# A hybrid decoder layer on eight cores: earlier norms, constant matmuls during the first load, and attention steps placed by estimated readiness

## What is computed

```python
h = rmsnorm(x, g_mix_pre); proj = h @ w_in
a_val, a_gate, q, k, v, f_logit = split(proj)
u = causal_depthwise_conv(a_val * sigmoid(a_gate), conv_w, conv_b)   # width 31
conv_out = silu(layernorm(u))
log_f = log_sigmoid(f_logit + b_forget); c = cumsum(log_f)
attn = softmax(q k^T / 8 + c_t - c_s, causal) @ v                    # 8 heads x 64
mix = concat(conv_out, attn) @ w_out
x = x + rmsnorm(mix, g_mix_post)
h = rmsnorm(x, g_ffn_pre)
y = (silu(h @ w_gate) * (h @ w_up)) @ w_down
x = x + rmsnorm(y, g_ffn_post)
```

## Time and profile before

| | |
|---|---|
| median of 3 runs | 2523.05 us (2521.86 to 2574.8) |
| the profiled execution | 2522.89 us |
| its span on the slowest core, 4 | 2521.3 us; the others 2503.7 to 2517.0 us |
| mean granted TensorE clock | 0.965 to 0.969 of 2.4 GHz |

### The profile page before, as it was taken

How to read it: one execution, slowest core, us unless ns; L and a number is a source line. 1 busy time by engine, 2 the same in 40 slices (tenths; PEclk the granted TensorE clock), 3 DMA queues, 4 the chain that set the end, 5 groups by cost and what they waited for, 6 DMA issues and landing times.

```text
span 2521.3 us, 53550 instructions; the slowest of 8 cores (2503.7 to 2521.3 us)
## 1 busy us (share of the span) xinstructions
PE 2282.3 (91%) x19680; PEld 1046.8 (42%) x19680; DVE 1064.8 (42%) x1645; ACT 1576.5 (63%) x1393; POOL 542.7 (22%) x901
## 2 busy tenths in 40 slices
PE   6888889999899779998999999999999899999895
PEld 2343434444344334443444444444444444444342
DVE  3545454455344543344234424424424332443643
ACT  2156567777676666676677677777767767772311
POOL 0231223132121421141013023013113201302301
PEclk9899999999899979999999999999999999998998
DMA  6765657577566765666635644554553464453542
GB/s 146 184 150 138 175 125 199 126 158 158 126 179 147 147 155 122 191 136 189 191 108 150 200 129 137 181 160 127 179 179 110 139 205 115 141 167 122 171 143 91
DMA packets 225324, 384.28 MB, mean 152 GB/s; under 512 B 34736, under 2 KB 152752, under 8 KB 222896
## 3 DMA queue, kind: packets, MB, share of 16 engines
q1 hardware_dynamic: 191840, 296.52, 40.5%
q0 software_dynamic: 33232, 84.34, 16.4%
HBM read 350.19 MB, written 72.55 MB: 168 GB/s over the span
## 4 chain that ended last, share of the span: by engine, by line
PE 67%; ACT 11%; DVE 7%; issue 6%; DMA 4%; POOL 2%; SPq 1%; DVEq 0%; ACTq 0%; POOLq 0%
PE pbig L372 67%; ACT s_pt L1076 5%; DVE s_tmp L860 2%; SPq L344 1%; ACT L384 1%; DVE s_x L862 1%; DMA s_xs<-xT 1%; DMA s_kr<-k_s 1%; ACT s_rstd L384 1%; DVE s_hT L465 1%; ACT s_sq L478 1%; ACT s_pt L1081 1%; DMA conv_s<-s_cvst 1%; DMA v_s<-s_vst 0%; POOL s_pt L1085 0%
## 5 line engine op out<-in xcount | busy, mean ns | idle before, releaser
L1076 ACT ACTIVATE s_pt<-pbig,s_bias 128x2048 bf16<-128x2048 f32 x512 | 1005.9, 1965 | 440.2 <-PE pbig L372 434.2
L372 PE MATMUL pbig<-s_h,s_wr 128*128 128x512 bf16 x2816 | 697.4, 384 | 11.5 <-DVE s_sa L908 10.8
L372 PEld LDWEIGHTS pbig<-s_vr,s_pt 128*128 128x128 bf16 x8832 | 349.3, 99 | 166.8 <-issue 50.9
L372 PE MATMUL pbig<-s_vr,s_pt 128*128 128x65 bf16 x8832 | 371.4, 195 | 18.9 <-DVE s_atok L1116 8.6
L372 PEld LDWEIGHTS pbig<-s_h,s_wr 128*128 128x128 bf16 x2816 | 245.5, 98 | 335.6 <-issue 116.4
L372 PE MATMUL pbig<-s_qr,s_kr 64*128 64x512 bf16 x1024 | 312.9, 386 | 77.5 <-ACT s_pt L1076 56.1
L908 DVE SCALAR_TENSOR_TENSOR s_sa<-s_th,pbig 128x512 f32<-128x512 f32 x176 | 120.8, 686 | 491.4 <-ACT s_th L907 487.4
L372 PE MATMUL pbig<-s_qw,s_kr 64*128 64x512 bf16 x1024 | 314.4, 388 | 0.0
L1085 POOL TENSOR_SCALAR_AFFINE_SELECT s_pt<-s_pt 128x128 bf16<-128x128 bf16 x256 | 84.9, 331 | 929.5 <-ACT s_pt L1081 904.1
L372 PE MATMUL pbig<-s_actA,s_wr 128*128 128x512 bf16 x1024 | 256.9, 381 | 1.5 <-DVE s_mix L941 1.1
L409 POOL TENSOR_TENSOR s_ssA<-s_ssA,s_sqr 128x512 f32<-128x512 f32 x112 | 154.9, 1383 | 459.9 <-ACT s_sqr L402 455.6
(11 more groups left out here) (142 smaller groups left out, 2274.5 us busy)
## 6 DMA issues: line engine op xcount, KB each, us to landing
s_wr<-wg_b SPq DMA_DIRECT2D x88, 512.0 KB, 3.9
s_wr<-wu_b SPq DMA_DIRECT2D x88, 512.0 KB, 4.4
s_wr<-wd_b SPq DMA_DIRECT2D x128, 352.0 KB, 3.2
s_vr<-v_s SPq DMA_DIRECT2D x288, 130.0 KB, 3.4
s_kr<-k_s SPq DMA_DIRECT2D x448, 64.0 KB, 3.9
s_xs<-xT POOLq DMA_DIRECT2D x48, 512.0 KB, 6.5
...
```

The source lines that it names most:

```text
L372: P.op("pe", lambda e: e.matmul(out, lhsT=lhsT, rhs=rhs, start=start, stop=stop, **kw), reads=reads, writes=[wkey])
L1076: P.op("act", lambda e: e.activation(out=p[:], in_=pbig[:, 0:4, :], func=AF.Exp, bias=bias[:, c, h:h + 1], scale=1.0), reads=bk + bias.key ...
```

## The change

The planner gets a model of time. `_Cost` is a stand-in engine with a duration for each kind of instruction (for example 512 / 2400 + 0.0025 us for a full-size bf16 matmul at one clock, 0.08 + columns / 1200 us for an activation). `_time` gives each recorded instruction an end from its engine's last end and its dependences' ends, each DMA a landing from one shared wire, 1.28 us for a change between Ln and Tanh on ScalarE and 0.097 us for a change of matmul kind. `ready` gives the time at which the dependences of keys are met:

```diff
+    def ready(self, eng, reads, writes):
+        t = 0.0
+        for d in self._deps(eng, reads, writes):
+            if d.is_dma:
+                t = max(t, self.landed[d.semkey])
+            elif d.eng != eng or eng != "pe":
+                t = max(t, d.done)
+        return t
```

A filler group yields 0.0 first, with its readiness in `fneed`; an attention step does the same in `need`. The loop uses both:

```diff
+    fneed = []
     def group(nk, lhs, rhs, out, reads, b, cost=MM, step=4):
+        fneed[:] = [lambda: max(max(P.ready("pe", reads(k), ()) - cost * k for k in range(nk)), P.ready("pe", (), [PB(b)]))]
+        yield 0.0
         for k in range(nk):
             mm(out, lhs(k), rhs(k), k == 0, k == nk - 1, reads(k), PB(b))
```

```diff
                 for c in range(2 * j + 2):
+                    n = hpos[(j, h)] % NQ
+                    if c <= 2 * j:
+                        need[:] = [kring[upos[(j, h, c // 2)] % NKV].keys + qtwin[n].keys + qring[n].keys, [PB(i) for i in range(4)]]
+                    else:
+                        need[:] = [kdring[n].keys + qring[n].keys, [PB(i) for i in range(3)]]
+                    yield 0.0
                     yield qk(j, h, c)
                     if len(pend) > 1:
+                        p = pend[0]
+                        need[:] = [p[3].keys + vring[upos[(p[0], p[1], p[2] // 2)] % NKV].keys, [PB(4)]]
+                        yield 0.0
                         d = pv()
...
+        if c == 0.0:
+            t = fneed[0]()
+            while fa[2] > -DEBT and t > P.free["pe"] + 0.15 and need and P.ready("pe", need[0], need[1]) < t - 0.3:
+                s = a_step()
+                if s is None:
+                    break
                 fa[2] -= s
             continue
         if isinstance(c, tuple):
...
         rem_f = max(A_END * f_total - fa[0], 1.0)
         rate = min(R_MAX, (a_total - fa[1]) / rem_f)
-        fa[2] = min(fa[2] + rate * c, 2.0)
+        fa[2] = min(fa[2] + rate * c, CAP)
         while fa[2] > 0:
+            if need and fa[2] < CAP - 0.3 and P.ready("pe", need[0], need[1]) > P.free["pe"] + 0.1:
+                break
             s = a_step()
             if s is None:
                 fa[2] = 0
```

Constant matmuls during the first load, chunk 0's norm written out, and norms of chunks 1 to 3 inside `p_kv(i)`, after the third V group (EARLY = 2):

```diff
+    def norm_early(i):
         flush("sq")
         b = bank()
         yield from stats(sq, 8, b)
         norm_tail(b, rstd, 1.0 / D)
-        defer("h", [scale_by(xs, V_GPRE, rstd, hT[i % 3], k) for k in range(8)], 2, every)
+        def one(k):
+            def f():
+                scale_by(xs, V_GPRE, rstd, hT[i % 3], k)()
+                if k % 2 and i < 3:
+                    x_piece(i + 1, k // 2, "sp")
+            return f
+        defer(("h", i), [one(k) for k in range(8)])
+        if i == 3:
+            defer("x", [lambda g=g: bulk.append(("x", lambda: x_piece(4, g))) for g in range(4)], 6, 2)
...
-        flush("h")
+        b = bank()
+        hold = Rot(4)
+        def idle(n):
+            for _ in range(n):
+                h = hold.next()
+                mm(pb[h][:], ones_bf[:], pt[0][:, 0, :], True, True, ones_bf.keys + pt[0].keys, PB(h))
+        idle(8)
+        for k in range(8):
+            P.op("act", lambda e, k=k: e.activation(out=sq[:, k, :], in_=xs[:, k, :], func=AF.Square), reads=[xs.keys[k]], writes=[sq.keys[k]])
+            mm(pb[b][:], ones_bf[:], sq[:, k, :], k == 0, k == 7, ones_bf.keys + [sq.keys[k]], PB(b))
+            idle(10 if k == 2 else 2 if k < 7 else 8)
+        norm_tail(b, rstd, 1.0 / D)
+        for k in range(8):
+            scale_by(xs, V_GPRE, rstd, hT[0], k)()
         load_x(1)
         ld("pool", identb, identb[:], cst_d[:, 0, :])
         yield from p_kv(0)
-        yield from norm_fin(1)
-        flush("h")
...
-        yield from norm_fin(2)
-        flush("h")
-        load_x(3)
-        wl("q", winQ, 0, C_Q, C_K, hT[2].keys[7:8])
-        wl("g", winG, 0, 0, C_Q, hT[2].keys[7:8])
+        flush_h(2)
+        wl("q", winQ, 0, C_Q, C_K, hT[2].keys[0:1])
+        wl("g", winG, 0, 0, C_Q, hT[2].keys[0:1])
...
+            if hp == 3 and i < 3:
+                norm_sq(i + 1)
...
+            if tb == EARLY and i < 3:
+                yield from norm_early(i + 1)
```

The first FFN chunk (j = 0) takes eight bf16 squares to TensorE for both norms; its residual has g_mix_post already in mix:

```diff
+            if j == 0:
+                P.op("dve", lambda e, b=b, ob=ob: e.tensor_scalar(out=mix[:, ob, :], in0=pb[b][:], scalar1=V(V_GPOST + ob), scalar2=None, op0=ALU.mult),
+                     reads=[PB(b)] + vecs.keys, writes=[mix.keys[ob]])
+                P.op("act", lambda e, b=b, ob=ob: e.activation(out=sq[:, ob, :], in_=pb[b][:], func=AF.Square), reads=[PB(b)], writes=[sq.keys[ob]])
+                continue
...
+        yield from stats(*((sq, 8, b) if j == 0 else (hlA, 2, b)))
         norm_tail(b, rstd, 1.0 / D)
-        defer("x1", [resid(mix, V_GPOST, X, ob) for ob in range(8)], 2, 1 if j == 0 else 2)
-        defer("x1", sq_steps(X, 8, ssA, hlA), 4, 1 if j == 0 else 2)
+        if j == 0:
+            def first(ob):
+                eng, T = ("pool", ssV) if ob > 5 else ("dve", tmp[ob % 2])
+                def f():
+                    P.op(eng, lambda e: e.tensor_tensor(out=T[:], in0=mix[:, ob, :], in1=rstd[:], op=ALU.mult), reads=[mix.keys[ob]] + rstd.keys, writes=T.keys)
+                    P.op(eng, lambda e: e.tensor_tensor(out=X[:, ob, :], in0=T[:], in1=X[:, ob, :], op=ALU.add), reads=T.keys + [X.keys[ob]], writes=[X.keys[ob]])
+                return f
+            def square(k):
+                return lambda: P.op("act", lambda e: e.activation(out=sq[:, k, :], in_=X[:, k, :], func=AF.Square), reads=[X.keys[k]], writes=[sq.keys[k]])
+            defer("x1", [first(ob) for ob in (0, 6, 1, 2, 7, 3, 4, 5)], 1)
+            defer("x1", [square(k) for k in range(8)], 4)
+            return
+        defer("x1", [resid(mix, V_GPOST, X, ob) for ob in range(8)], 2, 2)
+        defer("x1", sq_steps(X, 8, ssA, hlA), 4, 2)
...
+        yield from A3(0)
         yield ("att", 2.0)
-        yield from A3(0)
-        yield ("att", 3.0)
         for j in range(NOWN):
```

For the last own chunk the V staging is a smaller buffer, vst2, with 8 instead of 12 blocks, 4 instead of 8 decay steps, and its store is shorter; sqr and ssA are now outside it:

```diff
-    vst = [OV("vst0", [128, NH, 12, 65], BF16, w4), OV("vst1", [128, NH, 12, 65], BF16, tmp[0])]
-    ust.append(OV("ust2", [128, CH], BF16, hlA, 1, 1024))
-    assert hlA.off + 1024 >= vst[1].off + vst[1].size
+    vst = [OV("vst0", [128, NH, 12, 65], BF16, w4), OV("vst1", [128, NH, 12, 65], BF16, tmp[0]), OV("vst2", [128, NH, 8, 65], BF16, tmp[0])]
+    ust.append(OV("ust2", [128, CH], BF16, ssA, 1, 1024))
+    assert ssA.off + 1024 >= vst[1].off + vst[1].size and sqr[0].off >= vst[2].off + vst[2].size
+    vst_of = lambda j: vst[0 if j == 0 else 2 if j == NOWN - 1 else 1]
```

141 lines of the change are left out of this document (106 added, 35 removed).

## The result

The changed kernel takes 2467.14 us (median of 4 runs, 2463.09 to 2468.23), the kernel before 2521.86 us (3 runs, 2520.8 to 2523.05): ratio 0.978, 95% interval 0.9761 to 0.9799. That is faster, 55 us of the 99 forecast. It is inside the range, outside the likeliest case (2400 to 2455), and 3 us under the window of rival (a). In some executions of these kernels (one of the kernel before, 2574.8 us) the cores of one half of the chip, or all eight, had a lower mean granted clock, down to 0.80, and took up to 12% longer; times and ratios here are those of the other executions, of which e5 and e8 have one each and so no ratio.

What follows compares the result with a forecast made beforehand. TensorE, busy 91%, was taken as the bound, with only its idle time and low clock to win. Terms -11 - 28 - 42 - 13 - 19 - 4 + 2.7 + 15 = -99 gave 2424 us from 2522.9; range 2372 to 2484.

Steps and rivals of the forecast that it cites:

- rival (a): Planner's picture of time drifts, part 4 only trades one wait for another: 2470 to 2485 us, chance 0.21.
- Parts 1 and 2: Start of the kernel: constant matmuls plus early norms for chunks 1 to 3, -11 us (bounds -3 to -15).
- Part 2: Early norms, chunks 1 to 3: -5.4 us, -0.6 for clock, and -3.5 from a V evacuation wait that goes.
- The constant matmuls: During the first load: higher clock for the three stats matmuls and first groups, -1.5 us (bounds +1 to -3).
- Part 3: First FFN chunk: v_s store wait gone, shorter A2 to A3 chain, fewer forced attention units; -28 us, 60% of 47.
- Part 4 in the own chunks: Attention by readiness in 100:850: half of 84.1 us idle and of 27 us clock, -42 and -13 us.
- Part 4 in the FFN: Attention by readiness in 1000:2280: 40% of 48 us idle, -19 us, and -4 us of clock.
- The penalty: +15 us for what the planner cannot know: low clock, late loads, attention put ahead of a truly ready group.
- (b): Rival: readiness does nearly all, upper bounds throughout, no penalty; 135 us saved, 2388 us, chance 0.14.
- (c): Rival: put-off steps pile up before a chunk's need mark, where no filler runs; slower, 2573 us, chance 0.04.
- (d): Rival: a denser TensorE draws a lower clock, and the gain is given back; 2583 us, chance 0.01.
- What would show it: Signs: idle before 2280 about 115 us, s_pt waits below 45, stats within 14 us after the A2 tail, among others.

Runs made afterwards that it cites:

- e5: The changed kernel without the constant matmuls during the first load: 2467.17 us (one run).
- e8: The changed kernel with a credit cap of 12 instead of 4, so more attention steps may be put off: 2488.35 us (one run).
- e6: The changed kernel with norms of chunks 1 to 3 between the chunks again and the old order of loads: 2474.82 us, ratio 0.9825.
- e7: The changed kernel with the first FFN chunk's norms and residual as before, freed buffers kept: 2456.56 us, ratio 0.9698.
- e12: The changed kernel with the large V staging buffer and its overlay as before, new norms kept: 2466.17 us, ratio 0.979.
- e10: The changed kernel with full attention steps' exponentials over 1024 of 2048 columns, half the probabilities left out: 2390.43 us, ratio 0.9438.
- e1: The changed kernel with both readiness rules off and the credit cap back at 2.0: 2500.24 us, ratio 0.9879.

## Why the prediction was right, and where its sizes were off

**What bounds the kernel** held. TensorE's busy time changed by 5.6 us (2282.3 to 2276.7), with some 9.4 us of constant matmuls added (92.1 us busy to own chunk 0, 82.6 in e5), so on the other work it fell by 15; the gain is in idle time and clock.

**Parts 1 and 2** (-11) gave 6.6. Part 2 is right in mechanism and gave some 6 of its 9.5 (e6). The constant matmuls (-1.5) gave nothing (e5): the step that failed is that the higher clock would last into the 24 matmuls that nothing else paces; it was there for the eight before them, where VectorE sets the pace. Chunk 3's K group starts at 91.0 (median; 92.0 on the slowest core), not near 89. The 5 us of low clock that I took for 0:100 from the 0.93 are too few, for the reason given with the stretches.

**Part 3** (-28) gave 25, so the sum came out by luck: its reason was not right. I built the 60% on the v_s store and on the chain from A2 to A3. e7 and e12 show that neither matters by itself. The sentence on the forced units, which I had beside it, carries it as far as the rows go. The chain got shorter (19.4 us instead of 23), but a chain beside enough other matmuls is no path.

**Part 4 in the own chunks** (-42 idle, -13 clock) is the term that failed: idle fell by 11.7 us, from 77.3 to 65.6, where I took half of 84.1. The clock's share was near: PE busy fell by 27.6 us, of which 15 steps are 17.3 and 10 are left. The half was taken of all idle time, though beside the 6.3 us for `s_qr` (gone) the rows named only two kinds of wait, exponentials and squares. These were 35.0 us before in this stretch and are 19.6 after (medians), so nearly half of them did go, 15.4 us. Of the other waits the deferred step added 7.9 us (`s_cs`), which the rules don't see, and those for `s_atok` grew from 2.7 to 6.5. "While the other had matmuls to give" doesn't hold for those waits; why so much of the named ones stayed is argued, not shown: a stall of the filler is filled only while a step is ready, and steps become ready one per exponential. And the forecast had no term for steps put off, 17 of the 40 us by which the stretch got shorter.

**Part 4 in the FFN** (-19, -4) gave 5. I had read 27.3 us of waits for exponentials as a matter of order. They grew there, from 22.3 to 29.1 (medians), with the steps put off into this stretch. e10 shows that they are one of length: half the activation takes away two thirds of the idle time there.

**The penalty** (+15) covered a part of these two. It was to stand for low clock and late loads; of loads little came (TensorE's waits for `s_u` are 4.5 us in all, for `s_kr` 4.0, against 8.3 for `s_kr` and 6.3 for `s_qr` before).

**The rivals.** (a) comes nearest in time (2470 to 2485 for 2467), yet its reason, a picture that drifts, isn't what happened: the rules are worth 31 us (e1), not "a few". What is true of it is that waits were traded, as `s_sq` for `s_cs`. (b) is refuted: the measured time is 79 us above its 2388. (c) acts from a larger cap on (e8: at A1(0) 32 us ahead, of which the 20 steps put off are 23, so truly 9 ahead, and 24 behind at the end) and at cap 4 costs no more than the last burst. (d) is refuted in the profiled executions, more strongly than before: with half exponentials all cores are dense for 1.1 ms, each with clock 1.00 (the slowest core's row).

```profile
1000.00:2140.00 1140.00, 1127.41 (x10406) 550.77 (x10404) 453.22 (x664) 589.44 (x674) 237.31 (x282) 1.00 0.55 159
```

98.9% busy at clock 1.00. The Trainium skill (TensorE: Matmul & The Clock Gate, Seeing it yourself) warns of 13/16 of the clock here; this row doesn't agree.

**What would show it.** Right: PE busy (5.6 us less, though only because the constant matmuls fill what they fill), no wait for s_qr at the second chunk, the clock of 100:850 (0.97, forecast 0.98), no growth of waits for loads. Wrong: waits for s_pt, the idle time before A1(7), 153 us by the table and not 115, and the 14 us after the tail.
